# 32 more tokens leave the dense U products of a PEER layer, their rows gathered four slots side by side

## The reference

```
q      = x @ w_q                          # 8 heads x 2 halves x 128
scores = q . sub_keys                     # 128 keys a half
top 16 of each half, then top 16 of the 16 x 16 sums  -> experts (of 128 * 128), gates = softmax
act    = gelu(u[experts] . x)             # per token 8 x 16 = 128 slots
ffn    = sum over slots of gates * act * v[experts]
x      = layer_norm(alpha * x + ffn)
```

## Time and profile before

| | |
|---|---|
| median of 3 runs | 3270.34 us (3270.07 to 3271.58) |
| the profiled execution | 3272.12 us, span 3270.3 us |
| TensorE busy | 3173.4 us, 97% of the span |
| TensorE weight loads | 2886.0 us, 88% |
| VectorE busy | 2537.1 us, 78% |
| ScalarE busy | 1306.9 us, 40% |
| GpSimd busy | 1958.6 us, 60% |
| moved by DMA | 765.22 MB, 234 GB/s over the span |

### The profile page before, as it was taken

One profiled execution on the slowest core, in us unless ns is written; L12 is line 12 of the kernel. 1 busy time (PEld: TensorE's weight loads), 2 busy tenths in 40 slices (PEclk: granted clock), 3 DMA queues, 4 the chain that ended last, 5 costly groups with the idle time before them and its releaser, 6 DMA issues. The chain is left out here.

```text
span 3270.3 us, 64230 instructions
## 1 busy us (share of the span) xinstructions
PE 3173.4 (97%) x18582; PEld 2886.0 (88%) x18582; DVE 2537.1 (78%) x5431; ACT 1306.9 (40%) x2080; POOL 1958.6 (60%) x1556
## 2 busy tenths in 40 slices
PE   8998999999999999999999999999999999999997
PEld 8878889999999888888798787999999998888886
DVE  1475658888888899999925746588888888999998
ACT  2464234444444333333324643344444443333332
POOL 3454348888654466666545543488885535666665
PEclk9999999999999999999999999999999999999999
DMA  4002139999787699999820021499997867999996
GB/s 162 36 2 78 54 107 321 319 320 319 244 297 252 245 338 337 339 335 335 281 103 26 2 78 61 131 320 319 321 319 243 290 241 276 338 338 337 337 333 225
DMA packets 249405, 765.22 MB, mean 234 GB/s; under 512 B 28384, under 2 KB 95712, under 8 KB 241376
## 3 DMA queue, kind: packets, MB, share of 16 engines
q1 hardware_dynamic: 170400, 459.95, 42.6%
q0 software_dynamic: 73728, 268.47, 22.0%
q10 hardware_dynamic: 5184, 35.65, 3.1%
HBM read 677.98 MB, written 85.98 MB: 234 GB/s over the span
## 5 line engine op out<-in xcount | busy, mean ns | idle before, releaser
L705 POOL TENSOR_TENSOR st_lo<-st_raw,st_hi 128x1024 fp32r<-128x1024 f32 x290 | 698.1, 2407 | 463.2 <-ACT st_hi L979 457.4
L979 ACT CAST st_hi<-st_raw 128x1024 fp32r<-128x1024 f32 x544 | 569.9, 1048 | 662.9 <-PE ps L2096 638.0
L2005 PE MATMUL ps<-t_hi,st_hi 128*128 128x384 f32 (+1 forms) x2288 | 794.4, 347 | 0.0
L2006 PE MATMUL ps<-t_lo,st_hi 128*128 128x384 f32 (+1 forms) x2288 | 786.2, 344 | 0.0
L813 POOL TENSOR_TENSOR wt_lo<-w_f,wt_hi 128x384 fp32r<-128x384 f32 x256 | 417.9, 1633 | 319.5 <-ACT wt_hi L1110 319.4
L2009 PE MATMUL ps<-t_hi,st_lo 128*128 128x384 f32 (+1 forms) x2288 | 462.6, 344 | 0.0
L2005 PEld LDWEIGHTS ps<-t_hi,st_hi 128*128 128x128 f32 x2288 | 430.0, 188 | 10.2
L2006 PEld LDWEIGHTS ps<-t_lo,st_hi 128*128 128x128 f32 x2288 | 430.1, 188 | 10.0
L2009 PEld LDWEIGHTS ps<-t_hi,st_lo 128*128 128x128 f32 x2288 | 408.5, 188 | 10.9
L1022 ACT ACTIVATE h_out<-ps 128x384 f32<-128x384 f32 x256 | 125.9, 492 | 695.4 <-PE ps L2009 614.5
L2096 PE MATMUL ps<-st_hi,wt_hi 128*128 128x512 f32 x1536 | 390.6, 390 | 2.7 <-ACT wt_hi L1110 2.7
(11 more groups left out here) (222 smaller groups left out, 4969.1 us busy)
## 6 DMA issues: line engine op xcount, KB each, us to landing
st_raw<-in_peer_u SPq DMA_DIRECT2D x256, 512.0 KB
st_raw<-in_peer_v SPq DMA_DIRECT2D x256, 512.0 KB
gelu_d<-h_out SPq DMA_DIRECT2D x256, 192.0 KB
h_in<-gelu_d SPq DMA_DIRECT2D x256, 192.0 KB
gates_d<-g_stage ACTq DMA_DIRECT2D x32, 1024.0 KB
g_ch<-gates_d SPq DMA_DIRECT2D x56, 512.0 KB, 6.1
w_raw<-in_w_in SPq DMA_DIRECT2D x16, 1168.0 KB, 5.3
st_raw<-in_peer_w_q SPq DMA_DIRECT2D x32, 512.0 KB
```

Source lines behind the costliest of these rows:

```text
L705: nc.gpsimd.tensor_tensor(st_lo[:, s].rearrange("p c f -> p (c f)"), st_raw[:, r], st_hi[:, s].rearrange("p c f -> p (c f)").bitcast(F32), ...
L979: nc.scalar.copy(st_hi[:, r % 2].rearrange("p c f -> p (c f)"), st_raw[:, r]).then_inc(st_h, 1)
L2005: nc.tensor.matmul(dst, st_hi[:, s, c], t_hi[:, c, rows], start=c == 0, stop=False)
L2006: nc.tensor.matmul(dst, st_hi[:, s, c], t_lo[:, c, rows], start=False, stop=False)
```

## The change

The last 32 tokens (480 to 511, `XT`) leave the dense U products, which become 352 columns wide (`TU`). Their map, and the V products, stay as they are: the activations of these tokens are put into the gates instead, and `h_in` is 1 there.

Their 128 slots are gathered with 32 tokens x 4 slots on the 128 partitions, so that 32 more gathers and dots of the same size do (`XR`), 160 instead of 128 in a layer (`DOTS`). For this ScalarE issues four small DMAs that bring the numbers into that order (`idx`), and four that repeat the tokens' `x` four times (`x_x`). The dots are in bodies 0 to 7, eight instead of four in each (`BDOTS`); bodies 0 to 3 do the rest of the sparse block's slots, bodies 4 to 7 the new ones. Between them VectorE copies `x_x` into `x_ps`. The gathers still use the four slots of `b_row`; two gathers now follow each `st_lo` block.

After body 8 ScalarE takes GELU of the new dots and issues four DMAs that bring them back (`h_x`); VectorE multiplies them with their gates (`e_x`) after body 9, TensorE transposes the result before body 10, ScalarE copies 32 columns into `g_t`, and VectorE's last body waits for them. The third of the free banks holds that transpose and is opened before body 11 instead of body 8. The one-hot rows are made by VectorE as before.

```diff
+XT = 32
+XG = P // XT
+XR = SLOTS // XG
+DOTS = SLOTS + XR
+TU = TN - XT
+BDOTS = 8
+B_ROUNDS = (DOTS - U_ROUNDS * URING) // BDOTS
+X_BODY = (SLOTS - U_ROUNDS * URING) // BDOTS
...
-                nc.scalar.activation(h_out[:, s], ps[:, s, 0:TN], ACT.Gelu).then_inc(gelu_done, 1)
+                nc.scalar.activation(h_out[:, s, 0:TU], ps[:, s, 0:TU], ACT.Gelu).then_inc(gelu_done, 1)
...
-                stationary(m + QB // 2, s, ps[:, s, 0:TN], slice(P, T))
+                stationary(m + QB // 2, s, ps[:, s, 0:TU], slice(P, P + TU))
```

GpSimd's order in a body:

```diff
             def body_blocks(t, half, more=True):
 
-                for k in range(UDOTS):
-                    rest_block((QB + b_body) // 2 + 2 * t + k // 2, (QB + b_body + k) % RAW)
+                for k in range(2):
+                    rest_block((QB + b_body) // 2 + 2 * t, (QB + b_body + k) % RAW)
+                    for n in range(2):
+                        gather_b(t, half, UDOTS + 2 * k + n)
+                for k in range(2):
+                    rest_block((QB + b_body) // 2 + 2 * t + 1, (QB + b_body + 2 + k) % RAW)
                     if k == 0 and more:
                         numbers_b(t + 1, 1 - half)
-                    if k > 0 and more:
-                        gather_b(t + 1, 1 - half, k - 1)
-                if more:
-                    gather_b(t + 1, 1 - half, UDOTS - 1)
+                    for n in range(2 if more else 0):
+                        gather_b(t + 1, 1 - half, 2 * k + n)
```

ScalarE, after its three copies of the transposes, and in the bodies from 8 on (`n` counts them):

```diff
+            act.wait_ge(x_numbers, l + 1)
+            for g in range(XG):
+                act.dma_start(idx[g * XT:(g + 1) * XT, SLOTS:DOTS],
+                              idx_x[P - XT:P, g * XR:(g + 1) * XR]).then_inc(s_xn, 16)
+            for g in range(XG):
+                act.dma_start(x_x[g * XT:(g + 1) * XT], x_tok[P - XT:P, TB - 1]).then_inc(s_xx, 16)
...
+                        if n == 2:
+                            act.wait_ge(x_tr, l + 1)
+                            nc.scalar.copy(g_t[:, TU:TN], ps[:, FREE_BANKS[2], P - XT:P]).then_inc(x_set, 1)
...
+                        if n == 0:
+                            act.wait_ge(dots_kept, KEPT * (l + 1))
+                            nc.scalar.activation(dots[:, SLOTS:DOTS], dots[:, SLOTS:DOTS], ACT.Gelu).then_inc(x_gelu, 1)
+                            act.wait_ge(x_gelu, l + 1)
+                            for g in range(XG):
+                                act.dma_start(h_x[P - XT:P, g * XR:(g + 1) * XR],
+                                              dots[g * XT:(g + 1) * XT, SLOTS:DOTS]).then_inc(s_xh, 16)
```

VectorE, after the gates and in the bodies:

```diff
+            step.done(nc.vector.tensor_copy(e_x[:], e_all[:, UNITS - PH:UNITS].rearrange("p u k -> p (u k)")))
+            step.done(nc.vector.scalar_tensor_tensor(out=idx_f[:], in0=i_all[:, 0, (UNITS - PH) * TOPK:UNITS * TOPK],
+                                                     scalar=float(NK), in1=i_all[:, 1, (UNITS - PH) * TOPK:UNITS * TOPK],
+                                                     op0=ALU.mult, op1=ALU.add))
+            step.wait()
+            nc.vector.tensor_scalar(idx_x[:], idx_f[:], e_base[:, 0:1], None, ALU.add).then_inc(x_numbers, 1)
...
-                    if with_dots and g % 2 == 1:
-                        k = g // 2
-                        dve.wait_ge(s_brow[k], 16 * (B_ROUNDS * l + body + 1))
+                    if with_dots:
+                        k = g % UDOTS
+                        dve.wait_ge(s_brow[k], 16 * (BDOTS // UDOTS * (B_ROUNDS * l + body) + g // UDOTS + 1))
...
-            with dve.Fori(0, B_ROUNDS) as body:
+            with dve.Fori(0, X_BODY) as body:
                 one_hots(body, True)
-            with dve.Fori(B_ROUNDS, WIN * BODIES) as body:
+            dve.wait_ge(s_xx, 16 * XG * (l + 1))
+            step.done(nc.vector.tensor_copy(x_ps, x_x[:]))
...
+            with dve.Fori(X_BODY, B_ROUNDS) as body:
+                one_hots(body, True)
+            with dve.Fori(B_ROUNDS, B_ROUNDS + 2) as body:
                 one_hots(body, False)
+            dve.wait_ge(s_xh, 16 * XG * (l + 1))
+            nc.vector.tensor_tensor(e_x[P - XT:P], e_x[P - XT:P], h_x[P - XT:P], ALU.mult).then_inc(x_weights, 1)
+            with dve.Fori(B_ROUNDS + 2, B_ROUNDS + 3) as body:
+                one_hots(body, False)
+            dve.wait_ge(x_set, l + 1)
+            dve.sem_inc(waited, 1)
+            with dve.Fori(B_ROUNDS + 3, B_ROUNDS + 4) as body:
+                one_hots(body, False)
+            nc.vector.memset(h_in[:, :, TU:TN], 1.0)
```

TensorE, from body 8 on:

```diff
-            open_sums(FREE_BANKS).then_inc(acc_open, 1)
-            with pe.Fori(B_ROUNDS, WIN * BODIES - 1) as body:
+            open_sums(FREE_BANKS[0:2]).then_inc(acc_open, 1)
...
+            with pe.Fori(B_ROUNDS, B_ROUNDS + 2) as body:
+                late_body(body)
+            pe.wait_ge(x_weights, l + 1)
+            nc.tensor.transpose(ps[:, FREE_BANKS[2], 0:P], e_x[:], ident[:]).then_inc(x_tr, 1)
+            late_body(B_ROUNDS + 2)
+            assert WIN * BODIES == B_ROUNDS + 4
+            pe.wait_ge(x_set, l + 1)
+            open_sums(FREE_BANKS[2:3]).then_inc(acc_open, 1)
```

More of the change, by code:

```diff
@@ L286, in build @@
     idx_f = sp_r.tile("idx_f", [P, SLOTS], F32)
-    idx = sp_r.tile("idx", [P, SLOTS], U32)
+    idx = sp_r.tile("idx", [P, DOTS], U32)
+    idx_x = sp_r.tile("idx_x", [P, SLOTS], U32)
+    e_x = sp_r.tile("e_x", [P, SLOTS], F32)
+    h_x = sp_r.tile("h_x", [P, SLOTS], F32)
     idx_u = sp_r.tile("idx_u", [P, 2, URING], U32)
     idx_v = sp_r.tile("idx_v", [P, 2, VRING], U32)
-    idx_b = sp_r.tile("idx_b", [P, 2, UDOTS], U32)
+    idx_b = sp_r.tile("idx_b", [P, 2, BDOTS], U32)
     e_sp = sp_r.tile("e_sp", [P, SLOTS], F32)
     dot_8 = sp_r.tile("dot_8", [P, URING], F32)
-    dots = sp_r.tile("dots", [P, SLOTS], F32)
+    dots = sp_r.tile("dots", [P, DOTS], F32)
     w_sp = sp_r.tile("w_sp", [P, SLOTS], F32)
@@ L309, in build @@
     w_f = vp.tile("w_f", [P, 2, TN], F32)
+    x_x = nc.alloc_sbuf_tensor_at("x_x", [P, D], F32, offset=vp.end)
+    assert vp.end >= tk.end and D <= 4 * TN
     wt_hi = vp.tile("wt_hi", [P, 2, TN], F32R)
@@ L371, in build @@
     idx_b_set = sem("idx_b_set")
+    x_numbers, s_xn, s_xx, x_gelu, s_xh, x_weights, x_tr, x_set = (sem(n) for n in (
+        "x_numbers", "s_xn", "s_xx", "x_gelu", "s_xh", "x_weights", "x_tr", "x_set"))
     s_brow = [sem(f"s_brow{r}") for r in range(UDOTS)]
@@ L787, in _ @@
                 gather_b(0, 0, k, first=True)
-            with pool.Fori(0, B_ROUNDS // 2 - 1) as i:
+            body_blocks(0, 0)
+            body_blocks(1, 1)
+            pool.wait_ge(s_xn, 16 * XG * (l + 1))
+            pool.sem_inc(waited, 1)
+            with pool.Fori(1, B_ROUNDS // 2 - 1) as i:
                 for half in range(2):
@@ L1104, in _ @@
             act.wait_ge(dots_kept, KEPT * (l + 1))
-            nc.scalar.activation(dots[:], dots[:], ACT.Gelu).then_inc(h_sp, 1)
+            nc.scalar.activation(dots[:, 0:SLOTS], dots[:, 0:SLOTS], ACT.Gelu).then_inc(h_sp, 1)
             def round_gated(b, s):
@@ L1496, in _ @@
             step.wait()
-            nc.vector.tensor_scalar(idx[:], idx_f[:], e_base[:, 0:1], None, ALU.add).then_inc(idx_ready, 1)
+            nc.vector.tensor_scalar(idx[:, 0:SLOTS], idx_f[:], e_base[:, 0:1], None, ALU.add).then_inc(idx_ready, 1)
             dve.wait_ge(idx_ready, l + 1)
-            step.done(nc.vector.tensor_scalar(e_base[:], e_base[:], float(NEXP), None, ALU.add))
             assert step.n == n_idx
@@ L1566, in one_hots @@
                                                        op0=ALU.mult, op1=ALU.add,
-                                                       accum_out=dot_8[:, k:k + 1]).then_inc(u_dot, 1)
+                                                       accum_out=dot_8[:, g:g + 1]).then_inc(u_dot, 1)
                 if with_dots:
-                    dve.wait_ge(u_dot, SLOTS * l + URING * U_ROUNDS + UDOTS * (body + 1))
-                    nc.vector.tensor_copy(dots[:, ds(URING * U_ROUNDS + UDOTS * body, UDOTS)],
-                                          dot_8[:, 0:UDOTS]).then_inc(dots_kept, 1)
+                    dve.wait_ge(u_dot, DOTS * l + URING * U_ROUNDS + BDOTS * (body + 1))
@@ L1572, in one_hots @@
+                    nc.vector.tensor_copy(dots[:, ds(URING * U_ROUNDS + BDOTS * body, BDOTS)],
+                                          dot_8[:]).then_inc(dots_kept, 1)
                     dve.wait_ge(dots_kept, KEPT * l + U_ROUNDS + body + 1)
                     dve.sem_inc(waited, 1)
-            assert GROUPS == 2 * UDOTS
-            with dve.Fori(0, B_ROUNDS) as body:
+            assert GROUPS == BDOTS == URING
+            with dve.Fori(0, X_BODY) as body:
                 one_hots(body, True)
-            with dve.Fori(B_ROUNDS, WIN * BODIES) as body:
-                one_hots(body, False)
+            dve.wait_ge(s_xx, 16 * XG * (l + 1))
@@ L1586, in _ @@
             dve.wait_ge(h_sp, l + 1)
-            nc.vector.tensor_tensor(w_sp[:], dots[:], e_sp[:], ALU.mult).then_inc(w_ready, 1)
```

(3 more changed lines are left out.)

31 lines of the change are left out of this document (17 added, 14 removed).

## The result

The changed kernel takes 3310.56 us, the median of 4 runs (3306.99 to 3317.29), against 3270.96 us of the kernel before on the same chip: a ratio of 1.0123 with an interval of 1.0106 to 1.0141. The forecast was 3300 us, in a range of 3285 to 3320. The profiled execution has a span of 3308.0 us, 37.7 us more than before.

A forecast was written before the change was run, and what follows sets the result against it. It took TensorE and VectorE as level in the zone and TensorE as the bound of bodies 0 to 7. Terms summed to 14.8 us a layer, 29.6 us for two, on 3270.34: 3300 us, range 3285 to 3320.

The forecast's parts named there:

- Product: Each U product, 384 to 352 columns: 161.6 ns, 14.4 ns less, 0.345 us a block.
- Zone: The 12 gather rounds: 1.4 us less a layer, only at the start; VectorE's selection keeps rounds at 28.24 us.
- Gates: Between zone and bodies: exponent 0.9 us earlier, slower transposes 0.9 us later, added VectorE steps hidden; 0 in all.
- Bodies with DMA: Bodies 0 to 7: +12.4 us a layer, VectorE the bound at 25.3 us a body, and +1.4 us for DMA.
- Late part: Bodies 8 to 11, up to V: +2.4 us a layer, of which +2.2 for ScalarE's GELU and four DMA issues.
- V's shift: The start of V in each layer: some 15 us later, from terms that sum to 14.8 us.
- TensorE everywhere: Rival: TensorE paced the zone and stays the bound everywhere, 3182 us; chance 0.04.
- DMA-bound bodies: Rival: the DMA engines become the bound of bodies 2 to 7, 27.0 us a body, 3318 us; chance 0.16.
- Late rows: Rival: gathered rows take 12 us instead of 5.8, +3.3 us a body in 16 bodies, about 3350 us; chance 0.05.

The follow-up runs named there:

- experiment 6: The changed kernel with the four DMAs of `h_x` issued by GpSimd instead of ScalarE: 3295.99 us.
- experiments 1 and 5: The kernel before with U products of 352 columns alone (3236.81 us) and of 256 columns (3195.59 us), leaving out the activations of the last 32 and 128 tokens.
- experiment 3: The changed kernel with all gathers kept, but four of the eight dots of a body replaced by one-column copies: 3270.53 us.
- experiment 4: The changed kernel with all 96 dots of the zone replaced by one-column copies, gathers kept: 3292.67 us.
- both repairs: The changed kernel with `h_x` brought back by GpSimd's queue and the zone's first gather after block 3 instead of block 5: 3286.71 us.
- half the tokens, with both repairs and four slots: The changed kernel with 16 tokens, six dots a body, both repairs, `x_x` early on GpSimd's queue and four row slots: 3242.41 us.
- the version with `x_x` early: The 16-token kernel with both repairs and three slots, its `x_x` DMAs moved behind the first three gathers of body 0: 3268.18 us.
- experiment 1: The kernel before with the 352-column U products alone, no added gathers or dots, activations of the last 32 tokens left out: 3236.81 us.

## Why the prediction was right, and where it was off

The mechanism was right: products shorter, zone unchanged, bodies handed from TensorE to VectorE. Term by term, in layer 0:

- *Product.* 161.6 ns forecast. In the zone a block takes 3.80 us (816.61 to 820.41), 158.3 ns a product; the 1.43 us of eight products run to the end of the last one, which itself takes 0.32. In the late part the groups take 1.49 us, about 167 ns a product. Without effect in the zone and bodies, since TensorE waits. The Trainium skill's formula, which the prediction weighed (TensorE: Matmul & The Clock Gate, Back-to-back issue gap), gives 149.2 ns; the trace doesn't agree.
- *Zone.* -1.4 forecast, -2.3 measured; rounds 28.33 us.
- *Gates.* 0 forecast, -2.5 measured. GpSimd and ScalarE are as idle as TensorE there. The exponent followed `c_all` at once and no longer 2.2 us behind it, for not only the block cast but also the table load of 1.28 us had gone from the path; the prediction had counted 0.9. The copy to `c_top` took 0.18 us; in the kernel before it took 1.22, beside an `st_lo` of GpSimd. Against that, the slow transposes cost 0.6 of the 0.9 us forecast. The four added steps hid behind ScalarE's copies, where a wait of 1.68 us is left.
- *Bodies with DMA.* +13.8 forecast, 1049.03 - 837.98 = 211.05 against 195.3, +15.7, measured. VectorE's floor was 25.39 for 25.28. The misses are small: 3.3 us of waits for rows, and one instruction, the copy of `dots` at the end of body 7. It took 1.78 us in this layer and 1.96 in the other; the seven before it took 0.17 to 0.20. Timelines of VectorE and GpSimd:

```profile
941.69 0.17 DVE L1612 COPY dots<-dot 128x8 f32 x1
...
1045.39 1.78 DVE L1612 COPY dots<-dot 128x8 f32 x1
```

```profile
1044.75 2.39 POOL L719 TENSOR_TENSOR st_lo<-st_raw,st_hi 128x1024 fp32r<-128x1024 f32 x1 [3.56 <-ACT st_hi L999]
```

GpSimd's operation ends at 1047.14 and the copy at 1047.17 us: it stood until GpSimd was done. In the kernel before, the slow copy to `c_top` ended in the same way, at 834.29, with an `st_lo` that ended at 834.25. The Trainium skill (SBUF — State Buffer, SBUF: two separate sides) says that VectorE and GpSimd share one pair of ports, which whoever starts first holds for the whole instruction, and that a float32 copy from SBUF to SBUF on VectorE, as this one is, is among those that need it; the trace agrees.

- *Late part.* +2.4 forecast, +7.6 measured: the mis-sized term. The prediction put a GELU and four DMA issues, at 0.35 to 0.5 us each from one row of another transfer, at 2.2 us. These cost 0.62 each, and with the stores behind them, the wait and the slow groups after it 6.4 us (experiment 6). Without them the part is 1.2 us longer than before, 0.7 in layer 1.

Together -2.3 - 2.5 + 15.7 + 7.6 = 18.5 against V's shift of 18.6 us; the forecast was 14.8. Layer 1 repeats it with 17.5. Two terms came out too low (bodies by 1.9, late part by 5.2 us) and two turned out better than forecast (zone by 0.9, gates by 2.5). That they cancel in part is luck: with the zone and the gates as forecast the two layers would have come to some 7 us more, close to the upper end of the range.

Of the rivals, TensorE everywhere fell with experiments 1 and 5. The DMA-bound bodies fell as the first bound: the bodies moved 351 GB/s, and 366 in experiment 3, above the 350 from which that rival was to decide and, the latter, above the 358 that the prediction cites; and experiment 3 found the next wall at 23.8 us. Late rows cost 3.3 us, not 3.3 a body. But experiment 4 showed how near the next bound of the zone lies, 1.2 us a round below VectorE: TensorE again, at its slower pace of 4.00 us a block, with GpSimd's order beside it. The prediction had put TensorE at 25.9 us a round (6.67 blocks of 3.875 us are 25.8).

## What to carry to other kernels

Work taken from the busiest engine pays only down to the next engine's floor in that stage, and what it pays for with another engine's time is charged in full as soon as that engine is the floor: size the trade so that the two end level, here at half the tokens, with both repairs and four slots (3242 us). When two engines are level, a late request hurts more than its bytes: look at when a gather is issued before blaming bandwidth. Cost each DMA issue on the queue of the engine that must issue it, and put it where that engine is idle.

## What the hardware showed unasked

- One and the same product ran at two paces with the granted clock at 1.0. TensorE's groups of eight products of 368 columns, in the version with `x_x` early and in the one with four slots:

```profile
604.59 1.49 PE L2082 MATMUL ps<-t_hi,st_lo 128*128 128x368 f32 x8
```

```profile
606.93 1.55 PE L2088 MATMUL ps<-t_hi,st_lo 128*128 128x368 f32 x8
```

A block thus takes 4.00 or 4.16 us; with 352 columns it was 3.80 us in the changed kernel and 4.00 in experiment 1, at about the same place. The profiled execution with four slots took 3255.66 us, while its four others took 3240.83 to 3247.83. Both paces also stand within one trace: in experiment 4 blocks start 4.00 us apart up to 619.59 us and 3.80 apart from 627.52 on. What sets the pace is open; no run was made for it. It can cost time where TensorE ends last: with four slots, at 4.16 us a block, the first one-hot came at 837.23 us, with three slots at 832.33.
- This wait of TensorE cost more than its length. After the 4.66 us the window of the changed kernel (columns as above) shows the clock at half, 1.2 GHz, and the two groups that took 3.78 us lie in it:

```profile
1075.00:1080.00 5.00, 4.82 (x21) 4.82 (x22) 2.50 (x7) 1.78 (x4) 0.00 (x0) 0.50 1.01 420
1080.00:1083.80 3.80, 3.80 (x26) 3.80 (x25) 1.63 (x6) 0.27 (x1) 0.00 (x0) 0.99 0.14 58
```

- Four small DMAs between SBUF regions cost ScalarE's queue 2.48 us and GpSimd's 2.06 us.
